# A two-block transformer kernel: first weight unit and half of X by quarters on two queues, later constants behind the third unit, the sine layers' full turns taken off on GpSimd

## The reference

```python
h = rmsnorm(x, norm_mix)                     # x * rsqrt(mean(x*x) + eps) * g
p = h @ w_in                                 # 2048 -> 512 + 3*768 + 2*768
y_a = multiscale_pool_mixer(p[..., :512], pool_w, pool_b, pool_scale)
# implicit filters of the second mixer, from 33 features of the 256 positions
f = sin(fr1 * (feat @ w1 + b1))              # 33 -> 64
f = sin(fr2 * (f @ w2 + b2))                 # 64 -> 64
h_fwd, h_bwd = split(f @ w3) * decay         # 64 -> 2*768
y_b = hyena_mixer(...)                       # width-3 convolution, gate, long convolution by Fourier sums
y_c = chunked_spatial_gating(...)            # gelu, layernorm, mixing over positions
x = x + concat([y_a, y_b, y_c]) @ w_out
```

## Time and profile before

| what | value |
|---|---|
| median of 3 runs | 2212.95 us (2211.09 to 2214.64) |
| the profiled execution, its own time | 2212.98 us |
| its span, first to last instruction | 2211.2 us |
| TensorE busy | 2182.3 us, 99% |
| VectorE, ScalarE, GpSimd busy | 1305.8, 1009.6, 50.9 us |
| chain that ended last, TensorE's share | 96% |
| mean granted TensorE clock | 0.997 |

### The profile page before, as it was taken

One profiled execution on the slowest core, in us unless ns is written; L12 is line 12 of the kernel. 1 busy time (PEld: TensorE's weight loads), 2 busy tenths in 40 slices (PEclk: granted clock), 3 DMA queues, 4 the chain that ended last, 5 costly groups with the idle time before them and its releaser, 6 DMA issues.

```text
span 2211.2 us, 27940 instructions
## 1 busy us (share of the span) xinstructions
PE 2182.3 (99%) x11714; PEld 1870.5 (85%) x11714; DVE 1305.8 (59%) x1586; ACT 1009.6 (46%) x1179; POOL 50.9 (2%) x75
## 2 busy tenths in 40 slices
PE   7999999999999999999999999999999999999998
PEld 6888788888888888888898889878888888888886
DVE  7757647777777776444655665456555555444444
ACT  5444436555555554344554444445333334333343
POOL 1030000000000000000001000000000000000000
PEclk9999999999999999999999999999999999999999
DMA  9554555665556555555576555546666665555552
GB/s 305 160 159 153 191 190 172 202 198 177 198 178 195 186 191 191 191 189 190 153 218 196 167 172 191 190 134 210 190 188 188 186 187 190 189 190 189 190 189 96
DMA packets 267871, 410.05 MB, mean 185 GB/s; under 512 B 6630, under 2 KB 246310, under 8 KB 249313
## 3 DMA queue, kind: packets, MB, share of 16 engines
q1 hardware_dynamic: 264672, 395.47, 54.7%
q0 software_dynamic: 2352, 11.47, 1.5%
q10 hardware_dynamic: 720, 1.32, 0.2%
HBM read 406.12 MB, written 2.11 MB: 185 GB/s over the span
## 4 chain that ended last, share of the span: by engine, by line
PE 96%; DVE 2%; DMA 1%; ACT 1%; issue 1%; DVEq 0%; SPq 0%; ACTq 0%
PE bank L1354 34%; PE bank L1367 17%; PE bank L1391 11%; PE bank L1396 11%; PE bank L1392 11%; PE bank L1357 2%; PE bank L1358 2%; PE bank L1369 2%; DMA raw<-in_w_in 1%; PE bank L1246 1%; ACT whi L400 1%; PE bank L1200 0%; DVE M L1136 0%; DVE wlo L687 0%; PE bank L1279 0%
## 5 line engine op out<-in xcount | busy, mean ns | idle before, releaser
L687 DVE TENSOR_TENSOR wlo<-raw,whi 128x2048 fp32r<-128x2048 f32 (+1 forms) x374 | 857.1, 2293 | 800.6 <-ACT whi L400 800.6
L400 ACT ACTIVATE whi<-raw 128x2048 fp32r<-128x2048 f32 (+1 forms) x374 | 715.9, 1916 | 819.6 <-PE bank L1396 440.6
L1354 PE MATMUL bank<-hh,whi 128*128 128x512 f32 x3392 | 825.3, 396 | 14.6 <-ACT whi L400 10.9
L1354 PEld LDWEIGHTS bank<-hh,whi 128*128 128x128 f32 x3392 | 626.4, 189 | 146.4 <-ACT whi L400 10.8
L1367 PEld LDWEIGHTS bank<-hh,wlo 128*128 128x128 f32 x3392 | 429.7, 188 | 17.5 <-DVE wlo L687 0.4
L1367 PE MATMUL bank<-hh,wlo 128*128 128x256 f32 x3392 | 435.0, 281 | 0.0
L1391 PE MATMUL bank<-whi,hh 128*128 128x512 f32 x1088 | 429.8, 395 | 2.2 <-DVE M L832 2.2
L1392 PE MATMUL bank<-whi,hh 128*128 128x512 f32 x1088 | 428.3, 394 | 0.0
L1396 PE MATMUL bank<-wlo,hh 128*128 128x512 f32 x1088 | 274.3, 394 | 0.0
L1391 PEld LDWEIGHTS bank<-whi,hh 128*128 128x128 f32 x1088 | 205.1, 189 | 51.0 <-issue 2.4
L1392 PEld LDWEIGHTS bank<-whi,hh 128*128 128x128 f32 x1088 | 205.1, 189 | 46.7
(11 more groups left out here) (221 smaller groups left out, 883.3 us busy)
## 6 DMA issues: line engine op xcount, KB each, us to landing
raw<-in_mlp_w SPq DMA_DIRECT2D x128, 1024.0 KB, 5.4
raw<-in_ffn_w_up SPq DMA_DIRECT2D x88, 1024.0 KB, 5.0
raw<-in_ffn_w_down SPq DMA_DIRECT2D x44, 1024.0 KB, 4.8
raw<-in_w_in SPq DMA_DIRECT2D x34, 1024.0 KB, 5.5
raw<-in_fox_w_in SPq DMA_DIRECT2D x32, 1024.0 KB, 5.3
raw<-in_fox_w_in SPq DMA_DIRECT2D x16, 1032.0 KB, 5.4
raw<-in_w_out SPq DMA_DIRECT2D x16, 1024.0 KB, 4.8
raw<-in_fox_w_out SPq DMA_DIRECT2D x16, 1024.0 KB, 4.7
```

What stands on the lines that cost most here:

```text
L400: e.activation(whi[i % RING][:, 0:n], raw[i % RAW][:, 0:n], ACT.Copy).then_inc(s_hi, 1)
L687: e.tensor_tensor(wlo[i % RING][:, 0:n], raw[i % RAW][:, 0:n], whi[i % RING][:, 0:n].bitcast(F), ALU.subtract).then_inc(s_lo, 1)
L1354: e.matmul(bank[b][:, :], wh[:, k, s], hh[:, kk, :], start=kk == 0, stop=False)
```

## The change

- **Start.** SP issues unit 0 in four quarters (two chunks of 256 columns each, semaphores `s_w0` and `s_raw[0]`), then unit 1, X 8 to 11, X 12 to 15, unit 2 and on. ACT issues the first 16 columns (the gains, `s_gmix`), X 0 to 7 in four quarters, and the other columns (`s_col`). ScalarE does for each quarter two `high` and a quarter of `whi`, VectorE two `low` and a quarter of `wlo`; TensorE waits by quarters in unit 0.
- ScalarE then does split 1, the eight other `high`, four squares, split 2, four squares. VectorE does split 1, eight `low`, adds 1 to 3, split 2, adds 4 to 7.
- TensorE runs 32 matmuls of ones with ones before unit 0. Nothing reads their result.
- **Loads.** POOL issues the identity, features and filter weights as before. `w3`, the Fourier table, the first decay and a scale come when unit 2 is done, the layer norm's tables when unit 6 is done, the pool weights and edges after the Fourier products.
- **Sine layers.** `filter1` moves behind unit 1, `filter2` behind unit 4; ScalarE's sines stand apart as `sine1` (entry 2) and `sine2` (entry 5). VectorE computes only the angle; GpSimd does the rest in nine instructions (`reduced_angles`), each waiting for the one before.

The core of the diff:

```diff
 SIDE = {
-    1: [("split", 4), ("spread", 0)], 2: [("total", 0)], 3: [("filter1", 0)], 4: [("first_r", 0)], 5: [("filter2", 0)], 7: [("filter3", 0)],
+    1: [("split", 4), ("filter1", 0), ("spread", 0)], 2: [("total", 0), ("sine1", 0)], 4: [("first_r", 0), ("filter2", 0)], 5: [("sine2", 0)],
...
 def sync(e):
-            e.dma_start(X[:, 0:4, :], A["x"][:, 0:4, :]).then_inc(s_x[0], 16)
-            load(0)
-            e.dma_start(X[:, 4:8, :], A["x"][:, 4:8, :]).then_inc(s_x[1], 16)
+            src = units[0][0]
+            for m in range(4):
+                e.dma_start(raw[0][:, 512 * m:512 * m + 512].rearrange("p (k c) -> p k c", k=2), src[:, 2 * m:2 * m + 2, :]).then_inc(
+                    s_w0[m] if m < 3 else s_raw[0], 16)
             load(1)
...
 def gpsimd(e):
+            def reduced_angles(n):
+                at = 8 * n
+                e.wait_ge(s_angle, n + 1)
+                e.tensor_scalar(fn, fa, 1.0 / (2 * math.pi), MAGIC, ALU.mult, ALU.add).then_inc(s_sine, 1)
+                e.wait_ge(s_sine, at + 1)
+                e.tensor_scalar(fn, fn, -MAGIC, None, ALU.add).then_inc(s_sine, 1)
+                for i, c in enumerate(TWO_PI):
+                    e.wait_ge(s_sine, at + 2 + 2 * i)
+                    e.tensor_scalar(fh, fn, -c, None, ALU.mult).then_inc(s_sine, 1)
+                    e.wait_ge(s_sine, at + 3 + 2 * i)
+                    e.tensor_tensor(fa, fa, fh, ALU.add).then_inc(s_sine, 1)
+                e.wait_ge(s_sine, at + 8)
+                e.tensor_scalar(fa, fa, 3.1415925, -3.1415925, ALU.min, ALU.max).then_inc(s_fa, 1)
...
-            for dst, src in ((fe[0:33, :], A["feat"]), (f1, A["filt"]), (w3, A["w3"]), (CS, A["cs"]), (wpool, A["pool_w"])):
+            for dst, src in ((fe[0:33, :], A["feat"]), (f1, A["filt"])):
+                e.dma_start(dst, src).then_inc(s_feat, 16)
+            reduced_angles(0)
+            e.wait_ge(s_unit, 3)
+            for dst, src in ((w3, A["w3"]), (CS, A["cs"])):
                 e.dma_start(dst, src).then_inc(s_const, 16)
             e.dma_start(decay, A["decay"][:, :, 0:384]).then_inc(s_decay, 16)
+            e.dma_start(f1s[:, :], A["fscale"]).then_inc(s_fscale, 16)
             e.wait_ge(s_sq, 8)
             e.wait_ge(s_lx, 16)
+            reduced_angles(1)
+            e.wait_ge(s_unit, 7)
...
 def scalar(e):
-            e.dma_start(cols[:, :], A["cols"]).then_inc(s_col, 16)
+            e.dma_start(cols[:, 0:KD], A["cols"][:, 0:KD]).then_inc(s_gmix, 16)
+            for q in range(4):
+                e.dma_start(X[:, 2 * q:2 * q + 2, :], A["x"][:, 2 * q:2 * q + 2, :]).then_inc(s_x[q], 16)
+            e.dma_start(cols[:, KD:NCOL], A["cols"][:, KD:NCOL]).then_inc(s_col, 16)
             e.wait_ge(s_ones, 1)
             sqrt_table()
-            e.wait_ge(s_col, 16)
+            e.wait_ge(s_gmix, 16)
+            for q in range(4):
+                s = slice(512 * q, 512 * q + 512)
+                e.wait_ge(s_x[q], 16)
+                high(q, "mix")
+                e.wait_ge(s_w0[q] if q < 3 else s_raw[0], 16)
+                e.activation(whi[0][:, s], raw[0][:, s], ACT.Copy).then_inc(s_hi0 if q < 3 else s_hi, 1)
+            done[0] = 1
+            split(1)
+            for q in range(4, 8):
+                e.wait_ge(s_x[2 + q // 2], 16)
+                high(q, "mix")
             for q in range(8):
-                e.wait_ge(s_x[q // 2], 16)
-                high(q, "mix")
-                if q == 1:
-                    split(0)
-                    square(0, piece(0))
-                    square(1, piece(1))
-                if q == 5:
-                    split(1)
-            split(2)
-            for q in range(2, 8):
                 square(q, piece(q))
+                if q == 3:
+                    split(2)
...
 def tensor(e):
+            e.wait_ge(s_ones, 1)
+            for _ in range(32):
+                e.matmul(bank[7][:, 0:P], onesr[:, :], onesr[:, :], start=True, stop=True)
             for u, g, half in groups(U_IN, len(IN_GROUPS)):
```

More of the change, by code:

```diff
@@ L228, in two_block_program @@
         s_hi, s_lo, s_unit = sem("s_hi"), sem("s_lo"), sem("s_unit")
-        s_x = [sem(f"s_x{q}") for q in range(4)]
+        s_x = [sem(f"s_x{q}") for q in range(6)]
+        s_w0 = [sem(f"s_w0{m}") for m in range(3)]
+        s_hi0, s_lo0, s_gmix, s_feat, s_pw = (sem(n) for n in ("s_hi0", "s_lo0", "s_gmix", "s_feat", "s_pw"))
         s_col, s_id, s_const, s_decay, s_fscale, s_edge, s_ln, s_bs, s_again, s_fox = (
@@ L354, in gpsimd @@
             e.wait_ge(s_pq, 8)
+            e.dma_start(wpool, A["pool_w"]).then_inc(s_pw, 16)
+            e.dma_start(edge[:, :], A["edge"]).then_inc(s_edge, 16)
             for i in range(4):
@@ L474, in side @@
                         root(7, r_2)
-                    elif what in ("filter1", "filter2"):
-                        o = what == "filter2"
+                    elif what in ("sine1", "sine2"):
+                        o = what == "sine2"
                         e.wait_ge(s_fa, 1 + o)
@@ L774, in conv, with angles @@
                     e.scalar_tensor_tensor(dst[:, 0:T - 1], src[:, 1:T], ws[2], dst[:, 0:T - 1], ALU.mult, ALU.add).then_inc(s_cv2, 1)
[L776 to L781, removed]
[L782 to L791 removed]
+            def angles(n):
+                e.wait_ge(s_fmm, n + 1)
+                e.wait_ge(s_col, 16)
+                e.tensor_scalar(fa, bank[4 + n][0:64, 0:T], col("filt", 2 * n, 64), col("filt", 2 * n + 1, 64), ALU.add, ALU.mult).then_inc(s_angle, 1)
             def filter3(n):
@@ L960, in side @@
                     elif what == "filter1":
-                        e.wait_ge(s_const, 80)
-                        sine(4, col("filt", 0, 64), col("filt", 1, 64))
+                        angles(0)
                     elif what == "first_r":
@@ L965, in side @@
                     elif what == "filter2":
-                        sine(5, col("filt", 2, 64), col("filt", 3, 64))
+                        angles(1)
                     elif what == "filter3":
@@ L1050, in joined @@
                 turned(3, gname)
-            e.wait_ge(s_col, 16)
-            for q in range(8):
-                e.wait_ge(s_x[q // 2], 16)
+            e.wait_ge(s_gmix, 16)
+            for q in range(4):
+                s = slice(512 * q, 512 * q + 512)
+                e.wait_ge(s_x[q], 16)
                 low(q, "mix")
-                if q == 1:
-                    split(0)
-                    add_square(1)
-                if q == 5:
-                    split(1)
-            split(2)
-            for q in range(2, 8):
+                e.wait_ge(*((s_hi0, q + 1) if q < 3 else (s_hi, 1)))
+                e.tensor_tensor(wlo[0][:, s], raw[0][:, s], whi[0][:, s].bitcast(F), ALU.subtract).then_inc(s_lo0 if q < 3 else s_lo, 1)
+            done[0] = 1
+            split(1)
+            for q in range(4, 8):
+                e.wait_ge(s_x[2 + q // 2], 16)
+                low(q, "mix")
+            for q in range(1, 8):
                 add_square(q)
+                if q == 3:
+                    split(2)
             for g, (kind, j, _) in enumerate(IN_GROUPS):
```

40 lines of the change are left out of this document (19 added, 21 removed).

## The result

The changed kernel takes **2215.93 us** (median of 20 runs, 2213.59 to 2217.68), the kernel before 2212.56 (20 runs, 2211.09 to 2214.64): 1.0016 times the time before, with a 95% interval of 1.0009 to 1.0022. It is 3.4 us slower, where 2212.3, a gain of 0.65, was forecast; 2215.93 lies inside the forecast's range, on the side of its rival (c), and the interval leaves out 1. The profiled execution took 2216.7 us (span 2214.9, mean granted clock 0.996).

What follows compares the result with a forecast made beforehand. TensorE bounds the kernel, with VectorE's chain meeting it at unit 4 and the sine, split and release loop holding unit 8. The profiled 2212.98 less 0.65 gained at unit 8 gives 2212.3 us; range 2207.4 to 2216.5.

Steps and rivals of the forecast that it cites:

- rival (c): Sine layers: GpSimd's reduction becomes the wait; no difference at 0.66 us an instruction, 2214.6 at 0.75; chance 0.25.
- T1: Layer 1's sine reduction on GpSimd: 5.6 us plus 0.5 for stops by VectorE's two-input convolution steps.
- T2: Layer 2's sine reduction on GpSimd: 5.6 us plus 2.3 for the stop by VectorE's low of weights 7.
- 0.5 for the six with one input: GpSimd's reductions: six one-input instructions of the nine a layer at 0.5 us each, since they read one input.
- The forecast's upper end: GpSimd's reduction of a layer: 9.4 us if two operations in one instruction are slow, 1.0 each.
- The 0.74 for the adds: GpSimd's reductions: the three two-input adds of a layer at 0.74 us each.
- the start's gain: Start: unit 1 gains 3.6 us, VectorE's chain to the root gives it back; unit 4 gains 0.5.
- TensorE's waits at units 1, 2 and 4: TensorE early on: waits of some 1.5, 1.1 and 2.0 us, adding to some 4.5.
- the landing of unit 1: Start: unit 1's weights land at 13.05 us, bounds 11.0 and 13.5; a second queue adds only in the ramp.
- VectorE stops GpSimd: Reductions: VectorE's work holds GpSimd, one-input instructions also; stops of 0.5 in layer 1, 2.3 in layer 2.
- Rival (a): GpSimd's one-input instructions are not held, or cost 0.35: second reduction ends by 56.5, time 2211.1; chance 0.20.
- the moved loads: Later constants, 1.3 MB, issued behind unit 2: priced at nothing, as they are needed by unit 7 and later.

Runs made afterwards that it cites:

- two_op: The changed kernel with a neutral second step, times 1.0, in GpSimd's four one-step instructions a layer; 2211.57 us, ratio 0.9994 to the kernel before.
- keep_clock14: The changed kernel with 14 unread 512-column matmuls ahead of filter3's wait for the second sine; 2214.15 us, ratio 1.0003 to the kernel before.
- start_only: The changed kernel's start and moved loads, with the sine layers wholly on VectorE at their old places; 2212.25 us, ratio 1.0000 to the kernel before.
- no_warm: The changed kernel without the 32 matmuls of ones; 2216.46 us, ratio 1.0015 to the kernel before.
- sine_only: The old start and loads, with the changed kernel's GpSimd reductions and places of the sine layers; 2217.25 us, ratio 1.0019 to the kernel before.
- sines_dve_new: The changed kernel with the whole sine reductions back on VectorE, at the change's new places; 2214.41 us, ratio 1.0007 to the kernel before.
- keep_clock: The changed kernel with 8 unread 512-column matmuls ahead of filter3's wait for the second sine; 2215.95 us, ratio 1.0010 to the kernel before.
- fused: The changed kernel with the magic constant's subtraction folded into each multiplication, eight two-step GpSimd instructions a layer; 2211.13 us, ratio 0.9995 to the kernel before.

## Why the prediction was wrong

The forecast put unit 8 at 63.7, by its own formula 33.2 + T1 + 11.5 + T2 + 4.9 with T1 = 6.1 and T2 = 7.9 (which is 63.6; the tenth is rounding). With the rows of the changed kernel the same formula reads 33.71 + 7.17 + 11.62 + 8.90 + 5.06 = 66.46, to be compared term by term.

- **The step that failed: "0.5 for the six with one input, since these read one input and not two."** Of the six, two have a second arithmetic step. These took 0.39 to 0.45 (one of them 2.25, stopped by VectorE), and the four with a single arithmetic step 0.84 to 0.90: more than a two-input add (0.72 to 0.74 here). In a layer this is 4 x 0.35 = 1.4 more, 0.2 less for the two quick ones, 0.3 more for handoffs of 0.08 instead of 0.05, and 0.4 less for stops: T1 and T2 are 1.1 and 1.0 longer than forecast, 2.1 of the 2.8 by which unit 8 came later. The forecast's upper end was tied to the wrong form: it feared 1.0 for instructions with two steps, and it was those with one that were slow. `two_op` shows it: with about 0.40 for all six (save the one that VectorE stops) unit 8 starts at 63.09 and the time is 2211.57. The 0.74 for the adds held.
- **The term that was missing: the clock.** No part of the forecast, rival (c) included, had a price for what follows a wait of TensorE. (c) is what happened: it has no difference at T1 + T2 = 14.75, and they were 7.17 + 8.90 = 16.07, which gives 1.3. The late sine was worth 1.6, near that, and 1.65 to 1.8 came on top through the clock (`keep_clock14`). The trace of before had such a price, behind the wait of 2.19 us at 253.67, but not among the rows that the forecast used.
- **Right: the start's gain is given back on VectorE.** Root forecast at 33.2, measured 33.53; unit 4 at 36.3, measured 36.85 (35.51 to 36.85 in the five kernels with this start); `start_only` equals the kernel before. But unit 8 started 1.1 earlier there, and the forecast laid its gain to the sines alone. TensorE's waits at units 1, 2 and 4, forecast to add to some 4.5, were none, 0.68 and 1.30: unit 0 ended at 15.9, near the 15.5 that the forecast gave for a slow pace, and unit 1 followed it at once, not at 14.95.
- **Right in the main: the landing of unit 1.** 13.05 within 11.0 and 13.5 was forecast, and in the profiled execution of the change ScalarE's split began with it at 13.96. That was the latest of the ten kernels with the new start: in the other nine it began at 12.63 to 13.56, around the 13.1 of the earlier trace rows. So the second queue brought nothing that can be told from the scatter. This agrees with the Trainium skill, DMA: Bandwidth & Descriptors (Issuing engines are not separate DMA queues), by which transfers issued from several engines run on the same 16 DMA engines. The first matmul was missed: it came at 7.88, not 6.4, since its weights' quarter was split at 6.40 to 7.01 and the matmuls of ones ran until about 8. By `no_warm` this cost nothing that shows in the time.
- **Right: VectorE stops GpSimd.** 2.3 was forecast for the low of weights 7; the first instruction of layer 2 took 2.25 against 0.40, a stop of 1.85. It took 2.25 or 2.26 in seven of the eight kernels with GpSimd reductions, and 2.38 in `sine_only`. The contention named by the Trainium skill, GPSIMD Engine Reference (Key points), is there for a one-input instruction too. Rival (a), that they are not held, falls.
- **Right: the moved loads cost nothing.** `start_only` has them and is at 1.0000; no wait for `w3` or the Fourier table appears in the changed kernel up to 200 us. That a cost of the loads and a gain of the start cancel there is not ruled out, since no run has one without the other.

## What to carry to other kernels

Work moved to an engine off the critical path is not free when the result comes back: it has to be shorter than the slack, and the slack is read where the result is waited for (here 0.66 us an instruction). Price an instruction by its form, steps and inputs, and measure one before moving nine; here the multiplication by one was worth 4.4 us. Price a new wait of TensorE at more than its length: behind the 1.44 us lost to the sine, the matmuls gave up about 1.7 more, and a wait of 2.2 us that stood in the kernel all along gave up 1.5 in some executions and nothing in others. Compare a small change by many runs: in two single traces that one wait can make a difference of 1.5 us.

## What the runs showed of the hardware

- GpSimd, 64 x 256 float32 in place or between two buffers: an instruction of scalars with two arithmetic steps 0.39 to 0.46 us, with one step 0.84 to 0.90, an add of two inputs 0.72 to 0.74 in the change; beside VectorE's convolution `sine_only` has 1.13 for one step and 0.97 for an add. On VectorE the two forms took 0.28 and 0.29. Why one step costs more than two no run here shows. The Trainium skill, GPSIMD Engine Reference (Performance pitfalls for Q7 kernels), gives 4 cycles an element to a chain of dependent float32 operations; at the page's 1.2 GHz that would be 0.85 us for 256 elements, an estimate. It lies at the measured time, but whether the one-step form runs such a chain was not tried.
- The granted clock fell to 0.50 behind a wait of 1.44 us followed by `filter3`'s matmuls (the change), of 1.68 (`sine_only`) and of 3.55 (`sines_dve_new`). It stayed at 1.00 behind a wait of 1.30 between two units (the change, unit 4), of 1.43 behind the sine matmul (`start_only`) and of 1.39 behind `filter3` (`keep_clock`, profiled execution). Behind one and the same wait of 2.28 us near 253 us it fell in `fused` and `keep_clock` and stayed in `two_op` and `keep_clock14`. So the length of the wait alone does not decide.
- A fall of the clock to 0.50 cost 1.5 to 1.7 us each time: 5.60 against 3.92 for sixteen matmuls at unit 8, 5.54 against 3.95 at unit 4 (`sines_dve_new`), 5.59 against 4.08 near 255 us. Only `sine_only` has more, 6.05.
- GpSimd slows VectorE too: beside the first reduction VectorE's L806 took 1.35 for two instructions, and 0.88 beside none (both in the change).
